# Dense matmuls of 512 columns in two passes of 256, and one pair of tiles scaled later, in two fused transformer blocks

## What is computed

```python
for l in range(2):                       # first block
    z = rms_norm(x, norm_mix[l]) @ w_in[l]
    ...                                  # attentions y_a, y_b
    merged = sigmoid(ga + bg_a) * (y_a @ w_proj_a[l]) + sigmoid(gb + bg_b) * (y_b @ w_proj_b[l])
    x = x + merged @ w_out[l]
    u = causal_dwconv(rms_norm(x, norm_ffn[l]) @ w_up[l], conv_w[l], conv_b[l])
    x = x + (silu(u[..., FF:]) * u[..., :FF]) @ w_down[l]
...                                      # second block, attention part
hn = rms_norm(h, norm2_g)
h = h + (silu(hn @ w_gate) * (hn @ w_up)) @ w_down
```

## Time and profile before

| | |
|---|---|
| median of 3 runs | 2321.73 us |
| lowest and highest | 2320.89 and 2324.02 us |
| the profiled execution | 2322.03 us |
| its span | 2320.1 us |
| TensorE busy | 2275.7 us, 98%, 11106 matmuls |
| weight loads busy | 1769.7 us, 76%, 11106 |
| POOL, DVE, ACT busy | 70%, 44%, 26% |
| mean granted TensorE clock | 0.998 |

### The profile page before, as it was taken

The page is one execution under the profiler, slowest core; times in us unless marked ns, Lnnn a source line. Parts: engine busy times, 40 slices in busy tenths (PEclk is TensorE's granted clock), DMA queues, the critical chain, the costliest instruction groups (busy, mean ns, idle before and its releaser), DMA issues.

```text
span 2320.1 us, 34416 instructions
## 1 busy us (share of the span) xinstructions
PE 2275.7 (98%) x11106; PEld 1769.7 (76%) x11106; DVE 1028.9 (44%) x2012; ACT 607.4 (26%) x1299; POOL 1621.2 (70%) x942
## 2 busy tenths in 40 slices
PE   7999999999999999999999999999999999999997
PEld 5666788878888876667888788888787777888886
DVE  5676644364214346775433643143544544110112
ACT  4334710231001232347102311012321853000001
POOL 6565577777777775655777777777766757777775
PEclk9999999999999999999999999999999999999999
DMA  6222023323232232220233223323372102323222
GB/s 210 73 74 101 20 91 91 100 85 97 91 98 93 91 102 64 79 104 20 82 99 92 91 90 95 95 90 99 130 222 91 34 22 95 92 91 100 90 91 90
DMA packets 61584, 212.62 MB, mean 92 GB/s; under 512 B 6344, under 2 KB 6728, under 8 KB 61328
## 3 DMA queue, kind: packets, MB, share of 16 engines
q1 hardware_dynamic: 54368, 194.38, 26.7%
q10 hardware_dynamic: 7088, 16.58, 2.1%
HBM read 208.78 MB, written 10.01 MB: 94 GB/s over the span
## 4 chain that ended last, share of the span: by engine, by line
PE 94%; DVE 2%; DVEq 1%; ACT 1%; POOL 1%; issue 1%; DMA 0%; ACTq 0%; SPq 0%; POOLq 0%
PE out_tile L531 79%; PE stat L704 3%; PE turned L684 2%; PE out_tile L877 2%; PE out_tile L1063 1%; PE stat L531 1%; PE out_tile L886 1%; PE out_tile L771 1%; DVEq L1540 1%; PE stat L684 1%; PE turned L657 1%; POOL w_lo L1999 1%; PE out_tile L895 0%; POOL w_hi L1993 0%; PE stat L623 0%
## 5 line engine op out<-in xcount | busy, mean ns | idle before, releaser
L531 PE MATMUL out_tile<-arena_r,w_hi 128*128 128x512 f32 (+1 forms) x5240 | 1641.0, 394 | 0.0
L531 PEld LDWEIGHTS out_tile<-arena_r,w_hi 128*128 128x128 f32 x5240 | 985.4, 188 | 230.5 <-issue 1.9
L531 PE MATMUL out_tile<-arena_r,w_lo 128*128 128x512 f32 (+1 forms) x2620 | 1042.6, 398 | 9.1 <-POOL w_lo L1999 6.6
L1993 POOL TENSOR_TENSOR w_hi<-weight_ring,cst 128x1024 fp32r<-128x1024 f32 x342 | 645.0, 1886 | 539.3 <-PE out_tile L531 473.7
L1999 POOL TENSOR_TENSOR w_lo<-weight_ring,w_hi 128x1024 fp32r<-128x1024 f32 x342 | 823.0, 2406 | 26.9
L531 PEld LDWEIGHTS out_tile<-arena_r,w_lo 128*128 128x128 f32 x2620 | 493.0, 188 | 151.4 <-issue 25.7
L1519 DVE TENSOR_TENSOR x<-out_tile,x 128x512 f32<-128x512 f32 x72 | 49.8, 691 | 360.1 <-PE out_tile L531 360.1
L1337 ACT ACTIVATE work<-out_tile,p 128x512 f32<-128x512 f32 x88 | 65.9, 774 | 410.2 <-PE out_tile L531 410.2
L1787 DVE SCALAR_TENSOR_TENSOR work<-out_tile,p,work 128x511 f32<-128x511 f32 x88 | 65.6, 745 | 222.9 <-ACT work L1337 222.9
L2038 POOL TENSOR_SCALAR work<-work,small 128x384 f32<-128x384 f32 (+3 forms) x108 | 56.1, 532 | 64.0 <-DVE small L1571 45.0
L1208 ACT ACTIVATE work<-work,small 128x384 f32<-128x384 f32 (+3 forms) x152 | 83.3, 559 | 37.0 <-DVE small L1564 37.0
(11 more groups left out here) (226 smaller groups left out, 1920.7 us busy)
## 6 DMA issues: line engine op xcount, KB each, us to landing
weight_ring<-stream SPq DMA_DIRECT2D x356, 512.0 KB, 3.5
arena<-bias_rows ACTq DMA_DIRECT2D x4, 2048.0 KB, 11.1
bias_rows<-bias_kept ACTq DMA_DIRECT2D x2, 2556.0 KB, 24.1
bias_rows<-bias_kept SPq DMA_DIRECT2D x1, 2556.0 KB, 15.0
x<-x_t SPq DMA_DIRECT2D x4, 512.0 KB, 9.2
arena<-w ACTq DMA_DIRECT2D x1, 2048.0 KB, 8.0
out_t<-arena SPq DMA_DIRECT2D x8, 256.0 KB, 2.2
cst<-consts SPq DMA_DIRECT2D x1, 576.0 KB, 14.2
```

The source lines that it names most:

```text
L531: ins = pe.matmul(out, l, r, start=start and n == 0, stop=stop and n == 2, **kw)
L1993: pool.tensor_tensor(blocks_of(w_hi[:, s % SPLIT, :], used), blocks_of(ring[:, s, :], used), cols(cst, C_ONE).unsqueeze(1).to_broadcast([P ...
```

## The change

Where a call of the helper has an output 512 wide, each of its three passes becomes two of 256: first the three passes over the first 256 columns, then the same three over the other 256, with the same stationary operands loaded again. The start flag, which lets the first write into a bank overwrite, stands on the very first pass alone; the stop flag on the last of each half; the signal that a weight tile has been begun leaves with the first pass, that of a finished tile with the last. Calls with another width are as before. Besides, in the last block the first gate pair is scaled after all eight normed chunks (`pair_at=DC`), not after chunk 3.

```diff
+        token_halves = (slice(0, S // 2), slice(S // 2, S))
...
             def matmul(out, lhs, rhs, start, stop, **kw):
...
-                for n, (l, r) in enumerate(((lhs[1], rhs[0]), (lhs[0], rhs[1]), (lhs[0], rhs[0]))):
-                    ins = pe.matmul(out, l, r, start=start and n == 0, stop=stop and n == 2, **kw)
-                    if state["begin"]:
-                        ins.then_inc(weights_begun, 1)
-                        state["begin"] = False
+                halves = token_halves if out.shape[-1] == S else (slice(0, out.shape[-1]),)
+                if len(halves) > 1:
+                    kw["skip_group_check"] = True
+                for h, at in enumerate(halves):
+                    for n, (l, r) in enumerate(((lhs[1], rhs[0]), (lhs[0], rhs[1]), (lhs[0], rhs[0]))):
+                        ins = pe.matmul(out[:, at], l, r[:, at], start=start and n == 0 and h == 0, stop=stop and n == 2, **kw)
+                        if state["begin"]:
+                            ins.then_inc(weights_begun, 1)
+                            state["begin"] = False
                 return ins
...
             norm_input(LAYERS * 3 * DC + DC, lambda k: cols(p2, P2_N2 + k), scale, h_ffn,
-                       lambda kept: scale_pair(B, 0, (("gate", 0), ("upp", 0)), kept))
+                       lambda kept: scale_pair(B, 0, (("gate", 0), ("upp", 0)), kept), pair_at=DC)
```

## The result

| | before | after |
|---|---|---|
| median of 6 runs each, taken together on one chip | 2321.99 us | 2288.14 us |
| lowest to highest | 2320.89 to 2324.02 | 2279.87 to 2301.80 |
| profiled execution (span) | 2322.0 (2320.1) | 2281.86 (2279.9) |
| ratio after / before, 95% interval | | 0.9855 [0.9839, 0.9871] |

The forecast was 2375 us, 2.3% slower, with a range from 2350 to 2404. The changed kernel is faster, by 1.5% in these runs, and its runs differ by 22 us where those of before differ by 3. The median of all twelve is 2298.9 us, 1.0% under before.

A forecast was written before the change was run, and what follows sets the result against it. TensorE's dense passes were taken to bound the kernel. To the 2321.7 us median, 52 for 7,700 split passes and 1.8 for the layer branch, less 1 for early splits, made +53: 2375 us, range 2350 to 2404.

The forecast's parts named there:

- What bounds the kernel: TensorE's dense passes (L531): changing their distance changes the time almost one to one; 7,700 replaced passes on the path.
- The counts: At L531, 8028 of 8373 passes are 512 wide and become 16056 of 256.
- The price of a half: Dense stages: two halves at the hidden layer's settled 120 ns cost 240.0 against 233.3, +6.7 ns per pass, 52 us.
- Rival 1: Every dense stage: narrow passes stay at their unsettled distance; 2324 us at 116.6 ns, 2283 at 114; chance 7%.
- Bounds: Dense stages: a pair of halves costs at least 222 ns, by the load distance, and at most 253, by 280-column passes.
- Rival 2: Dense stages: a half at 117.9 ns, as if a boundary had a small fixed price; 2343 us; chance 5%.
- The rule of the Trainium skill: Dense passes: distance of N/2.4 + 2.5 ns, so the split adds 2.5 ns per replaced pass, some 19 us.
- Rival 3: Inner loops (L926, L1092): doubled bodies fetched again at 24 turns, 2.2 us open each; +53, so 2428 us; chance 5%.
- The hole at the layer branch: Branch back to the second layer (L741): TensorE's idle hole grows by some 1.8 us, once, to near 2.3.
- Instruction supply: TensorE's queue: a load and matmul every 120 ns can be supplied, as one pair per 101 ns was delivered before.
- Part 2: Last block's first gate pair, scaled after all chunks: zero effect, at most 1 us once if wrong.
- GpSimd's wait: GpSimd, which splits the weights: its wait for TensorE grows by some 50 us.

The follow-up runs named there:

- e15: Changed kernel with the first of the first three products on each weight tile left whole at 512 columns; 2338.29 us, ratio 1.0066.
- e5: Changed kernel with halves of 272 and 240 columns in place of 256 and 256; 2364.40 us, ratio 1.0181.
- e14: Changed kernel run again, unchanged; six runs between 2280.27 and 2321.87 us.
- e2: Kernel before with only the later scaling of the last block's first gate pair, no split; 2322.15 us, ratio 1.0000.
- e10: Changed kernel with one wait ahead of each of the hidden layer's two runs, not one every three passes; 2297.19 us, one run.
- e6: Changed kernel whose hidden layer streams the normed input in its first 18 passes and uses its blocks as stationary in the last 30; 2299.69 us, one run.
- e12: Changed kernel with hidden-layer sums going by turns to two halves of the bank, and single dense tiles run half by half; 2320.96 us.
- e13: Changed kernel with the same block of w2 as stationary operand for the hidden layer's last 30 passes; 2280.57 us.
- e18: The kernel of e16 run again, unchanged; 2286.29 us, ratio 0.9846.
- e8: Changed kernel with the three passes of the first call on each weight tile left 512 wide; 2312.02 us, ratio 0.9957.
- e7: Changed kernel with the first of the three products of every call left whole, the other two split; 2340.49 us, ratio 1.0076.
- e16: Changed kernel with the first two of the first three products on each weight tile left whole; 2286.60 us, ratio 0.9847.
- e17: As e16, but with the two whole products only at every fourth weight tile; 2283.48 us, ratio 0.9834.
- e11: Kernel before with a long-met wait ahead of every three wide passes; 2323.25 us, ratio 1.0002.
- e9: Changed kernel with a long-met wait ahead of every three dense halves; 2285.85 us, ratio 0.9835.

## Why the prediction was wrong, point by point

- **What bounds the kernel**: right. The distance between two dense passes changed, and the time with it almost one to one: 40.6 us in the five long stretches, 40.2 in the span. The 7,700 on the path are about right as a count (the chain before holds 7,982 records of L531, at most 345 of them not 512 wide), but only the 6,114 in the long stretches took the new price; the rest changed by nothing net.
- **The counts**: right. 16401 records at L537, which is 8373 + 8028 (window over the whole span: `1909.64 (x16401)` busy).
- **The price of a half, the step that failed**: "So 120 is the settled value, and some narrow ones at the start are cheaper", and "I take the settled value, because the dense stages are thousands of passes long." The hidden layer's passes do settle at 120.0 ns, in every kernel of this document. Wrong was that a dense stage that lasts settles there too. No stretch of dense halves did, in up to 3,144 passes: in the changed kernel each long one stands at 113.3 or 117.8 throughout. Per pair +6.7 ns were forecast; -6.6 was measured in the low stretches and +2.3 in the high ones. The term of +52 us is -40.6 in the profile of the changed kernel; with all of the path at the high distance it would be 7,700 x 2.3 = +18, an estimate to which e15, all high, comes near at +16.
- **What was there to be read.** The run of the earlier trace rows begins irregularly: its starts taken one by one stand 116, 113, 116, 119, 119, 121, 116 and 118 ns apart before they hold at 120. The first four have a mean of 116, a little under the 117 to 118 that I worked out, and distances below 117 occur at exactly this width. That should have made the price of a half a range with several values. Rival 1's line through the wide rows, one end of which is a long dense stretch, has 116, between the two distances that came; the row of the right width, from a different layer, lies outside them. I gave the rival 7%.
- **Bounds**: both held. The lower one, 222 ns a pair by the load, is borne out by e5, where passes of 240 columns stand 112.9 ns apart in the mean and none in the last stretch under 110.
- **Rival 1** (a half near its unsettled distance, 2283 at 114): this is what the changed kernel does at its best, 2280. **Rival 2** (117.9, so 2343): this is what e15 does, 2338. The changed kernel mixes the two by stretches, which none of the cases allowed for. That the measured median lies near rival 1's time owes something to which stretches stood low in these runs; in e14 it lies near no change.
- **The rule of the Trainium skill** (TensorE: Matmul & The Clock Gate, "Back-to-back issue gap"), N/2.4 + 2.5 ns, gives 109.2 at 256 and 215.8 at 512, so a split that costs 2.5 ns. The traces have 113.3 or 117.8 and 233.3: the split saves 6.6 in low stretches, against the rule's sign, and costs 2.3 in high ones, near its size. I left out that the page gives the formula for a matmul by itself and calls it off for a stream with a load ahead of each, for which it has some 131 ns at 512 columns; the trace does not agree with that either, at 233.3.
- **Rival 3, code fetched again at inner loops**: right to discount. The branches take 208 ns as before, and the long stretches run across them without a hole. The packets of the instruction queue went from 75 to 120; that the longer code alone is the reason is likely and not shown.
- **The hole at the layer branch**: right, "near 2.3 us" forecast, 2.35 measured (1.8 to 2.4 in the other profiles of kernels with even halves).
- **Instruction supply**: right; a load and a matmul every 113 ns over 3,144 passes left no hole.
- **Part 2 at zero**: right, by e2 to within 0.1%.
- **GpSimd's wait** was forecast to grow by some 50 us and shrank by 42, which follows from the failed step.

**Open.** Why the hidden layer stands at 120.0: its waits (e10), which operand streams (e6) and its accumulation region (e12) are excluded. So is its bank, by the changed kernel's own trace. The last key tile (`last_keys`) goes into the same `stat[0]` as halves, in two runs of 24 passes (start us; every third pass reads w_lo):

```profile
1758.03 0.28 PE L537 MATMUL stat<-arena_r,w_lo 128*128 128x256 f32 x1
...
1759.73 0.28 PE L537 MATMUL stat<-arena_r,w_lo 128*128 128x256 f32 x1
...
1761.90 0.28 PE L537 MATMUL stat<-arena_r,w_lo 128*128 128x256 f32 x1
...
1763.67 0.28 PE L537 MATMUL stat<-arena_r,w_lo 128*128 128x256 f32 x1
```

Fifteen passes take 1.70 us in the first run and 1.77 in the second, 113.3 and 118.0 ns. What no run changed is that the hidden layer reads both operands from one tensor, `arena_r` (the profile names it alone: `stat<-arena_r`), where every dense half has one of them in w_hi or w_lo. That held in e6 and e13 too and is the rival left to test: a hidden layer with one operand copied out of `arena_r`. Why there are two distances for dense halves, and how one and two whole passes choose between them, was not found either; e15 to e18 show that they do, not how. That three whole passes turn the distance at each tile (e8) and one leaves it at 117.8 (e15) fits no simple count that I know of. The kernel before, nearly all of whose dense passes are wide, alternates between starts of 236 and 231 ns and spreads by 0.2% at full clock.

## What to carry to other kernels

Price a pass by rows of the same kind of stage, and when a width shows two distances anywhere, carry both through the sum: here they lie on either side of no change. When a change makes the times spread, look in the chain for the same stretch with the same count and different lengths; a median of three runs would have told anything from -1.8% to nothing. A pattern that fixes the better value can be worth as much again as the change: two whole passes at every fourth weight tile give 2280 to 2286 us (median 2283), where the plain split gives 2280 to 2322 (median 2299).

## What the runs showed of the hardware that I had not expected

- In steady stretches with weights stationary, starts stand 233.3 ns apart at 512 columns (1,572 passes), 173.4 at 384 (starts one by one in the index queries of the kernel before) and 113.3 at 256 in low stretches: 60 ns less for every 128 columns, and 6.7 less than in proportion to the columns. So at full clock two narrow passes can be faster than one wide one. e5's narrower passes, of 240 columns, leave this line (112.9 where it has 105.8), near the 111 ns between loads. A stretch of 87 wide token-major passes stands at 229.3 (19.95 us, kernel before), so the line is not a floor.
- Passes of 256 columns have three steady distances in these kernels, 113.3, 117.8 and 120.0 ns. One holds for up to 3,144 passes, 0.35 ms, and the next stretch may take another.
- Whole passes at the start of each weight tile select the distance of the halves behind them: one, 117.8 (e15; e7 has one in every call); two, 113.3 (e16, e18; e17 at every fourth tile); three, each by turns (e8). Why is open.
- Uneven halves (272 and 240) cost 238.9 ns a pair (e5), 12 more than even ones at 113.3.
- A wait that is met costs TensorE nothing measurable, at one per 700 ns (e11) or per 340 ns (e9).
